# The sparse attention stage of a fused two-layer kernel with other matmuls placed between its rounds

## What is computed

```python
q = (qg[..., :N_HEADS * dh] * (dh ** -0.5)).reshape(bsz, seq, G, HPG, dh)
gates = jax.nn.sigmoid(qg[..., N_HEADS * dh:])
s = jnp.einsum("bqghd,bngd->bghqn", qblk, k_cmp)      # 15 compressed keys
p_cmp = jax.nn.softmax(jnp.where(vis, s - slopes * dist, NEG_INF)) * vis
o_cmp = jnp.einsum("bghqn,bngd->bqghd", p_cmp, v_cmp)
...
p = jax.nn.softmax(s)                                  # selected keys, window keys
o = gblk[..., 0:1] * o_cmp + gblk[..., 1:2] * o_slc + gblk[..., 2:3] * o_win
return out @ w_o
...
mod = jax.nn.silu(c) @ w_ada[l] + b_ada[l]
```

## Time and profile before

| | |
|---|---|
| median of 3 runs | 1025.66 us (1024.62 to 1027.26) |
| profiled execution | 1025.58 us |
| its span | 1023.9 us, clock 0.981 |
| PE busy | 976.4 us, 95% |
| DVE busy | 693.7 us, 68% |
| ACT busy | 483.3 us, 47% |
| POOL busy | 82.0 us, 8% |
| HBM | 182 GB/s over the span |

### The profile page before, as it was taken

One profiled execution on the slowest core, in us unless ns is written; L12 is line 12 of the kernel. 1 busy time (PEld: TensorE's weight loads), 2 busy tenths in 40 slices (PEclk: granted clock), 3 DMA queues, 4 the chain that ended last, 5 costly groups with the idle time before them and its releaser, 6 DMA issues.

```text
span 1023.9 us, 19441 instructions
## 1 busy us (share of the span) xinstructions
PE 976.4 (95%) x7938; PEld 945.9 (92%) x7938; DVE 693.7 (68%) x1090; ACT 483.3 (47%) x698; POOL 82.0 (8%) x129
## 2 busy tenths in 40 slices
PE   4999999999999997889999999999999779999998
PEld 4999999999999996579999999999998779999998
DVE  4876777777777647967777777777875465444443
ACT  5344634444445415856444444437666454444441
POOL 6000000000000012320010010120000000000000
PEclk9999999999999988999999999989999889999999
DMA  9655748787745660027577768434344336565621
GB/s 272 199 199 200 254 152 290 237 287 248 244 144 173 215 238 1 1 64 257 174 250 264 268 233 301 142 101 150 119 145 165 117 131 201 171 197 172 197 90 41
DMA packets 131387, 186.98 MB, mean 183 GB/s; under 512 B 6272, under 2 KB 102656, under 8 KB 131328
## 3 DMA queue, kind: packets, MB, share of 16 engines
q1 hardware_dynamic: 123984, 159.82, 47.5%
q0 software_dynamic: 6912, 25.17, 7.1%
q10 hardware_dynamic: 432, 1.16, 0.4%
HBM read 185.09 MB, written 1.05 MB: 182 GB/s over the span
## 4 chain that ended last, share of the span: by engine, by line
PE 79%; DVE 10%; ACT 5%; DMA 3%; issue 2%; SPq 0%; DVEq 0%; ACTq 0%
PE ps L1726 55%; PE ps L1797 15%; PE ps L1724 2%; ACT g_hi L629 1%; DVE ada_acc L1140 1%; PE ps L1764 1%; DVE g_lo L1172 1%; ACT g_hi L693 1%; DMA g_raw<-in_a_w_in 1%; DVE g_lo L1075 1%; DMA g_raw<-in_b_w_qg 1%; DMA g_raw<-in_w_kv 1%; ACT e_even L823 1%; DVE d_lo L1126 1%; DVE e_even L1421 1%
## 5 line engine op out<-in xcount | busy, mean ns | idle before, releaser
L1726 PE MATMUL ps<-opa_hi,g_hi 128*128 128x256 f32 x1216 | 351.4, 289 | 19.3 <-DVE opa_lo L1112 12.2
L1726 PE MATMUL ps<-opa_lo,g_hi 128*128 128x256 f32 x1216 | 348.4, 286 | 0.0
L1726 PE MATMUL ps<-opa_hi,g_lo 128*128 128x256 f32 x1216 | 348.0, 286 | 0.0
L1726 PEld LDWEIGHTS ps<-opa_hi,g_hi 128*128 128x128 f32 x1216 | 237.3, 195 | 22.5 <-issue 20.1
L1726 PEld LDWEIGHTS ps<-opa_lo,g_hi 128*128 128x128 f32 x1216 | 237.4, 195 | 0.2
L1726 PEld LDWEIGHTS ps<-opa_hi,g_lo 128*128 128x128 f32 x1216 | 237.1, 195 | 0.0
L1172 DVE TENSOR_TENSOR g_lo<-g_raw,g_hi 128x2048 fp32r<-128x2048 f32 x56 | 128.4, 2292 | 74.9 <-ACT g_hi L693 74.9
L1075 DVE TENSOR_TENSOR g_lo<-g_raw,g_hi 128x2048 fp32r<-128x2048 f32 x57 | 130.6, 2290 | 47.1 <-ACT g_hi L629 46.5
L629 ACT ACTIVATE g_hi<-g_raw 128x2048 fp32r<-128x2048 f32 x57 | 108.8, 1910 | 87.1 <-PE ps L1726 79.6
L1797 PE MATMUL ps<-hid_hi,d_hi 128*128 128x256 f32 x528 | 147.8, 280 | 0.1
L1797 PE MATMUL ps<-hid_hi,d_lo 128*128 128x256 f32 x528 | 147.6, 280 | 0.0
(11 more groups left out here) (303 smaller groups left out, 1344.5 us busy)
## 6 DMA issues: line engine op xcount, KB each, us to landing
g_raw<-in_f_w_gu SPq DMA_DIRECT2D x44, 1024.0 KB, 8.8
ada_raw<-in_w_ada POOLq DMA_DIRECT2D x48, 512.0 KB, 5.2
d_raw<-in_f_w_down SPq DMA_DIRECT2D x22, 1024.0 KB, 5.2
g_raw<-in_w_in SPq DMA_DIRECT2D x14, 1024.0 KB, 7.9
g_raw<-in_w_gate SPq DMA_DIRECT2D x11, 1024.0 KB, 7.1
g_raw<-in_w_up SPq DMA_DIRECT2D x11, 1024.0 KB, 9.6
d_raw<-in_w_down SPq DMA_DIRECT2D x11, 1024.0 KB, 5.1
g_raw<-in_a_w_in SPq DMA_DIRECT2D x10, 1024.0 KB, 7.8
```

The costliest lines, as they stand in the source:

```text
L1726: mm = pe.matmul(pair(b)[:, a, :], wt[:, a * P:(a + 1) * P], xt, **st)
```

## The change

- The query steps QG+2 and QG+3 are cut into units of one tile k (6 matmuls) and put between scores, turns and values of pairs 0 to 2 (`query_units`). Both now write bank 6, and QG+3 waits for the evacuation of QG+2.
- The output steps WO and WO+1 are cut the same way: WO's units 0 to 3 between `values(6)` and `turn(7)`, then 4 to 6, `values(7)`, WO+1's units 0 to 6, WO's unit 7, WO+1's unit 7 (`out_units`). WO also writes bank 6.
- ACT and DVE split QG+3, WO and WO+1 at other places: WO in the third round, WO+1 after the last copies of a turn, ahead of the low parts of pairs 6 and 7.
- The modulation sums run in four pieces of 6 columns before `values(2)` to `values(5)`, in bank 7; DVE's `make_mod(0)` follows at the end of the seventh round.
- The compressed branch runs in two halves of 8 heads. The first is done by pair 0 and the second in the rounds of pairs 3 and 4.
- The transposes of a pair use two banks, 4 and 5: the last four go to bank 4 again, after ACT has copied the first four.
- The gate product moves to bank 6, the compressed keys and values to bank 7, and `e_even` and `pt_buf` to the place of the upper half of `ada_acc`.

The diff, cut to its core:

```diff
@@ -826,11 +830,22 @@
 
             exps(0, 0)
             exps(0, 1)
-            act.wait_ge(cs_shift, 1)
-            act.activation(ctmp, ctmp, ACT.Exp).then_inc(cs_exp, 1)
+            def compressed_exp(q):
+
+                act.wait_ge(cs_shift, q + 1)
+                act.activation(c_half(q), c_half(q), ACT.Exp).then_inc(cs_exp, 1)
+
+            def compressed_copy(q):
+
+                act.wait_ge(pct_done, q + 1)
+                act.activation(pct[:, q, :], ps[:, 6 if q else 7, 0:T], ACT.Copy).then_inc(pct_made, 1)
+
+            compressed_exp(0)
             for j in range(1, NH // 2 + 2):
                 if j < NH // 2:
                     exps(j, 0)
+                if j == 5:
+                    compressed_exp(1)
                 if j >= 2:
                     act.wait_ge(pv_done, 2 * j - 2)
                     act.activation(opa_hi[:, j - 2, :], ps[:, 7, 0:T], ACT.Copy).then_inc(opa_hi_made, 1)
@@ -839,13 +854,17 @@
                         act.wait_ge(pt_done, 3 * j - 2 + q)
                         if q == 0 and j >= 2:
                             act.wait_ge(pv_done, 2 * j - 2)
-                        act.activation(pt_buf[:, 512 * q:512 * q + 512], ps[:, 4 + q, :], ACT.Copy).then_inc(pt_copied, 1)
+                        act.activation(pt_buf[:, 512 * q:512 * q + 512], ps[:, 4 + q % 2, :], ACT.Copy).then_inc(pt_copied, 1)
                 if j < NH // 2:
                     exps(j, 1)
                 if j == 1:
-                    act.wait_ge(pct_done, 1)
-                    act.activation(pct[:, :, :].rearrange("p a n -> p (a n)"), ps[:, 7, :], ACT.Copy).then_inc(pct_made, 1)
-            split_g(WO + 1)
+                    compressed_copy(0)
+                if j == 3:
+                    split_g(WO)
+                if j == 5:
+                    compressed_copy(1)
+                if j == 8:
+                    split_g(WO + 1)
             product_and_gained(WO, 3, opb_hi, opb_hi_made, "f_norm", 8)
         if last_stage >= 4:
             ffn(1)
...
+            def compressed_shift(q):
+
+                x = c_half(q)
+                dve.wait_ge(cs_done, q + 1)
+                own(dve.tensor_tensor(x.rearrange("p (a h n) -> p a h n", a=TT, n=16),
+                                      ps[:, 6 if q else 4, 0:T].rearrange("p (a h n) -> p a h n", a=TT, n=16),
+                                      cmp_bias[:, :, NH2 * q:NH2 * q + NH2, :], ALU.add))
+                own(dve.tensor_reduce(c_max(q), c4(x), AX_X, ALU.max))
+                dve.tensor_tensor(c4(x), c4(x), c_max(q).unsqueeze(2).to_broadcast([P, 16, 16]),
+                                  ALU.subtract).then_inc(cs_shift, 1)
+
+            def compressed_factors(q):
+
+                x = c_half(q)
+                dve.wait_ge(cs_exp, q + 1)
+                own(dve.tensor_reduce(c_max(q), c4(x), AX_X, ALU.add))
+                own(dve.reciprocal(c_max(q), c_max(q)))
+                f = cfac[:, q, :]
+                f2 = f.rearrange("p (a h) -> p a h", a=TT)
+                gate0 = gates[:, :, :].rearrange("p a (h b) -> p a h b", b=3)[:, :, NH2 * q:NH2 * q + NH2, 0]
+                own(dve.tensor_tensor(f2, c_max(q).rearrange("p (a h) -> p a h", a=TT), gate0, ALU.mult))
+                own(dve.tensor_tensor(f2, f2, any_vis[:, :].unsqueeze(2).to_broadcast([P, TT, NH2]), ALU.mult))
+                dve.tensor_tensor(c4(x), c4(x), f.unsqueeze(2).to_broadcast([P, 16, 16]), ALU.mult).then_inc(cs_made, 1)
+
             shift(0)
             shift(1)
+            compressed_shift(0)
+            dve.wait_ge(gates_made, 1)
             normalize(0)
             normalize(1)
-            evac_q(3)
...
             for j in range(2, NH // 2 + 2):
                 for e in range(2):
                     if j < NH // 2 + 1:
                         normalize(2 * j - 2 + e)
+                    if j == 4 and e == 0:
+                        evac_q(3)
                     if j < NH // 2:
                         shift(2 * j + e)
-                if j >= 2:
-                    dve.wait_ge(opa_hi_made, 8 * A_FILL["attn"] + j - 1)
-                    dve.tensor_tensor(opa_lo[:, j - 2, :], ps[:, 7, 0:T],
-                                      opa_hi[:, j - 2, :].bitcast(F32), ALU.subtract).then_inc(opa_made, 1)
-            split_g(WO + 1)
+                    if j == 2 and e == 0:
+                        evac_q(2)
+                    if j == 5 and e == 0:
+                        compressed_factors(1)
+                if j == 3:
+                    split_g(WO)
+                if j == 4:
+                    compressed_shift(1)
+                if j == 8:
+                    split_g(WO + 1)
+                dve.wait_ge(opa_hi_made, 8 * A_FILL["attn"] + j - 1)
+                if j == 7:
+                    make_mod(0)
+                dve.tensor_tensor(opa_lo[:, j - 2, :], ps[:, 7, 0:T],
+                                  opa_hi[:, j - 2, :].bitcast(F32), ALU.subtract).then_inc(opa_made, 1)
             add_product(WO, opb_hi, opb_lo, opb_hi_made, B_FILL["n3"], opb_made, "f_norm", 8)
...
+            def query_units(first, n):
+
+                for u in range(first, first + n):
+                    s, k = QG + 2 + u // KT, u % KT
+                    if u == 0:
+                        pe.wait_ge(gates_made, 1)
+                    if u == KT:
+                        pe.wait_ge(g_evac, evacs(QG + 2))
+                    g_step(s, opb_hi, opb_lo, no_wait, ks=range(k, k + 1))
+
+            def out_units(s, first, n):
+
+                for k in range(first, first + n):
+                    if s == 0 and k == 0:
+                        pe.wait_ge(pct_made, 2)
+                    if s == 1 and k == 0:
+                        pe.wait_ge(pt_copied, PT_NSA)
+                    g_step(WO + s, opa_hi, opa_lo, a_filled("attn"), ks=range(k, k + 1))
+
+            query_units(0, 4)
+
+            def turn(j, e):
+
+                pe.wait_ge(scaled, 2 * j + e + 1)
+                x = e_of(2 * j + e)
+                for b in range(2):
+                    for n, lo in enumerate((512 + b * P, b * 256, b * 256 + P)):
+                        i = (2 * e + b) * 3 + n
+                        q = i // 4
+                        if i % 4 == 0 and (j >= 1 or q == 2):
+                            pe.wait_ge(pt_copied, 3 * j + 1 if q == 2 else 3 * j - q)
+                        mm = pe.transpose(ps[:, 4 + q % 2, i % 4 * P:(i % 4 + 1) * P], x[:, lo:lo + P], ident[:, :])
+                        if i % 4 == 3:
+                            mm.then_inc(pt_done, 1)
 
             def values(j):
 
+                if j in (0, 4):
+                    pe.wait_ge(pct_made, 1 + j // 4)
+                if j >= 1:
+                    pe.wait_ge(opa_made, 8 * A_FILL["attn"] + j)
+                if 2 <= j < 6:
+                    ada_sum(0, 6 * (j - 2), 6)
                 pe.wait_ge(pt_copied, 3 * j + 3)
-                if j == 0:
-                    pe.wait_ge(pct_made, 1)
-                else:
-                    pe.wait_ge(opa_made, 8 * A_FILL["attn"] + j)
                 v = HD * (j // 2)
...
-                        for a in range(TT):
-                            mm = pe.transpose(ps[:, 7, (2 * q + a) * P:(2 * q + a + 1) * P],
-                                              ctmp[:, a * T + q * P:a * T + (q + 1) * P], ident[:, :])
-                    mm.then_inc(pct_done, 1)
-                if j >= 1:
-                    values(j - 1)
-                if j < NH // 2:
-                    turn(j)
-            for s in range(4):
-                g_step(WO + s, opa_hi, opa_lo, a_filled("attn") if s == 0 else no_wait)
+            scores(1)
+            pe.wait_ge(cs_shift, 1)
+            query_units(4, 2)
+            turn(0, 0)
+            query_units(6, 1)
+            turn(0, 1)
+            query_units(7, 1)
+
+            scores(2)
+            compressed_turn(0)
+            query_units(8, 2)
+            values(0)
+            query_units(10, 1)
+            turn(1, 0)
+            query_units(11, 1)
+            turn(1, 1)
+
+            scores(3)
+            query_units(12, 2)
+            values(1)
+            query_units(14, 1)
+            turn(2, 0)
+            query_units(15, 1)
+            turn(2, 1)
+
+            pe.wait_ge(g_evac, evacs(QG + 2))
+            scores(4)
+            values(2)
+            turn(3, 0)
+            pe.wait_ge(g_evac, evacs(QG + 3))
+            compressed_scores(1)
+            turn(3, 1)
+
+            scores(5)
+            values(3)
+            turn(4, 0)
+            turn(4, 1)
+            compressed_turn(1)
+
+            for j in (5, 6):
+                scores(j + 1)
+                values(j - 1)
+                turn(j, 0)
+                turn(j, 1)
+
+            out_units(0, 0, 2)
+            values(6)
+            out_units(0, 2, 1)
+            turn(7, 0)
+            out_units(0, 3, 1)
+            turn(7, 1)
+            out_units(0, 4, 3)
+            values(7)
```

(5 more changed lines are left out.)

120 lines of the change are left out of this document (43 added, 77 removed).

## The result

The changed kernel took 1047.1 us (median of 4 runs, 1046.9 to 1049.4) beside 1026.4 for the kernel before: a ratio of 1.0216, interval 1.0196 to 1.0235, slower by 20.7 us where 8.3 were forecast. The profiled execution took 1046.97 us, its span is 1045.2.

What follows compares the result with a forecast made beforehand. PE was taken as the bound (95% busy), with DVE pacing up to the fourth round. WO+2 starting later (+3.8) and clock behind four waits (+4.5) gave +8.3 on 1025.66: 1034.0 us, range 1027.5 to 1040.

Steps and rivals of the forecast that it cites:

- Walking the new order: New order of the attention stage laid out with old durations: four long PE waits, WO+2 starting 3.8 us later.
- A: Before the sums of values(2): PE stands 5.6 us, as pair 1's low part follows the split of WO on DVE.
- B: In turn(4): PE stands 4.5 us for normalize(9), which DVE has behind the second compressed factors.
- C: Before unit 6 of WO: PE stands 3.9 us, as DVE splits WO+1 ahead of opa_lo of pair 6.
- D: Before WO+2: PE stands 3.8 us for its split, with one unit left after WO ends.
- What it removes: In the attention stage: 11.5 us of PE waits, as far as filled, and some 7 us of slow clock.
- The clock on top: Half clock behind the four waits: 1.5 us each for C and D, 0.75 each for A and B, +4.5 us.
- The bounds: Clock cost behind each of the four long PE waits: 0 to 3 us, so 0 to 12 in all.
- The rule beside the rows: No DVE or ACT instruction overtakes a waiting one; otherwise A, C and their clock (11.8 us) go, sum -3.5.
- (1): Rival: woven units make PE late at turn(2) and turn(7), splits are done, A and C go; 1022.2 us, chance 0.07.
- (2): Rival: no difference; the four waits don't lower the clock, DVE's early row is 2 us shorter; 1027.5 us, chance 0.07.
- (3): Rival: the clock falls for long, all four waits cost 3 us more each; 1041 us, chance 0.08.

Runs made afterwards that it cites:

- e1 to e4: The changed kernel with one edit each, taking out wait A, B, C or D in that order: 1031.1, 1038.1, 1040.2 and 1040.3 us.
- e1: The changed kernel with the split of WO moved earlier on ACT and DVE, which takes out wait A: 1031.1 us.
- e14: The changed kernel with the edits against waits A, C and D, so B alone is left: 1023.1 us.
- e5: The changed kernel with all four edits (splits of WO and WO+1, second compressed exp, order of the last units), so none of waits A to D left: 1019.5 us.
- e6: The changed kernel with the edits against waits A, B and C, so D alone is left: 1022.3 us.
- e18: The changed kernel with all four edits, two early waits filled, and ACT's second compressed copy before the exp of head 11: 1013.0 us.
- e17: The changed kernel run again unchanged, five runs beside the kernel before: 1044.0 us, ratio 1.0188.

## Why the prediction was wrong

The direction and the mechanism held; the size did not. Point by point, in its own order:

- *Walking the new order.* The waits came as 1.74, 0.47 and 2.25 in the early rounds (forecast 1.7, 0.8, 2.6), A 5.44 (5.6), B 3.05 (4.5), C 3.77 (3.9), D 3.81 (3.8). DVE's idle time before the split in the third round was 6.47 (over 6). e1 to e4 took each out by the order alone, as the walk said they arise. So the waits were not too few: the walked ones add up to 23.9 us with the one at values(4), and PE stood 20.8 in the stage.
- *Wait B* was walked 1.5 too long. The walk has DVE working in a row from 410.0 up to it. In fact DVE stands still for PE's second compressed scores, 3.75 us at 423.54 and, with those scores at the full clock, 1.55 in e1; so this chain starts at PE as well, and B lasted 3.04 to 3.06 us in each of the seven kernels that have it.
- *One more us at values(4)* did not show: at half clock PE was late there. It shows in e1, 0.95.
- *Sums at 1.1 a piece*: 1.43 at the full clock (425.61 to 427.04), 2.66 at half.
- *What it removes* was wrong in one place. The half clock of 373 to 380 was counted as gone with the block of sums. It came again, 374 to 381, behind the 1.74 us for the compressed keys, which the walk had: 3.4 us lost. No clock was charged to a wait under 2 us.
- ***The clock on top* is the step that failed**: +4.5 for the four waits. Measured in the profiled execution, as half of the busy us at half behind each: A 4.1 (413.7 to 422.0), B 6.5 (432.9 to 445.9), C 2.6 (464.6 to 469.8), D 1.6 (480.3 to 483.4): 14.8, and 18.2 with the early 3.4. That is 13.7 more than forecast. Three smaller terms stand beside it: 1.7 of slow clock at 353.7 to 357.1, ahead of the stage; 1.3 for four pieces of sums that take 1.43 and not 1.1; and the waits, 3.4 shorter than walked. 8.3 + 13.7 + 1.7 + 1.3 - 3.4 = 21.6, and the spans differ by 21.3; an agreement this close is luck, as single executions differ by more. I had priced A and B at half of what the clock cost behind the wait of 2.21 us, since DVE paces the rounds and would hide a slow PE. It doesn't: behind A and B PE is busy without a gap in the windows of 7.6 and 12.15 us. A round of 4.9 us at the full clock takes 9.8 at half, and its sums come on top, so it is longer than DVE's 6, and DVE waits for PE.
- *The bounds* were 0 to 3 us each from the nearest rows, 12 in all. A and B went to 4.1 and 6.5. The rows showed single waits, and none two of them 19 us apart with scores, values and transposes between; where B is the only long wait (e14), the cost behind it is 1.7, within the bound.
- *The rule beside the rows.* By the Trainium skill (PSUM — Partial Sum Buffer, Engine vs sequencer instructions) the queues of DVE and ACT are strictly first in, first out. The trace agrees: `opa_lo(1)` stood behind the waiting split for 9 us.
- *Rivals.* (1), that PE comes late enough for the splits, did not happen: PE came later than walked, and so did the splits, which start from PE's own turn. Its 1022.2 is near what e5 (1019.5) and e6 (1022.3) reached, but these moved the splits and the exp, which is another way to it. (2) fell on the clock. (3), 12 us of clock and 1041, was nearest and still short by 6. The Trainium skill (Perfetto Trace Analysis, Optimization Strategy) says that interleaving regimes with different busiest engines may help: e5 and e18 agree, by 6 and 13 us, once no order stands in the way.

## What to carry to other kernels

When work is woven into a pipeline of several engines, place each helper instruction (a split, an exp, an evacuation) by what waits behind it on its own engine, and put it into a gap that the trace shows; here four such placements were worth 25 to 28 us and turned a loss of 2% into a gain of 0.7%. Price a new wait as the wait and the clock behind it, and where several waits lie close together with short instructions between them, expect the clock to cost as much as the waits. Split the times of repeated runs by the mean clock before comparing them: in e6 single times scatter by 2.1 us (standard deviation) and their rests by 0.8, in e17 by 2.2 and 1.7.
